# The second block's shift and scale rows: loaded and summed during attention by GpSimd, not during the first mixture by VectorE

## The chip, the cores and the metric

The kernel runs on one core of a Trainium2 chip, as one launch. The metric is the device time of an execution in microseconds (us). A core has a matrix engine (TensorE, PE), three engines for elementwise work (VectorE or DVE, ScalarE or ACT, GpSimd or POOL), SyncE (SP), which here issues the DMAs, and 16 DMA engines that move data between HBM and the on-chip memory (SBUF). TensorE writes to eight PSUM banks, `ps[0]` to `ps[7]`.

## The reference

Two transformer blocks follow each other on 256 tokens of width D = 1024, all in float32. Cut to what matters here:

```python
def first_block(x, c, ...):
    mod = silu(c) @ ada_w + ada_b                 # 1024 -> 6 x 1024: sh1 sc1 g1 sh2 sc2 g2
    h = rmsnorm(x, norm_mix) * (1 + sc1) + sh1
    x = x + g1 * diff_attention(h, ...)           # 8 heads
    h = rmsnorm(x, norm_ffn) * (1 + sc2) + sh2
    x = x + g2 * hier_moe(h, ...)                 # 16 experts, 2 for each token
    return rmsnorm(x, norm_final)

def second_block(x, c_2, ...):
    mod = silu(c_2) @ ada_w_2 + ada_b_2           # sh1, sc1: the first 2 x 1024 columns
    xn = rmsnorm(x, mix_norm_g_2) * (1 + sc1) + sh1
    ...                                           # projections, sparse attention, RWKV
    h = h + gt2 * hier_moe(...)                   # 32 experts
```

The change is about sh1 and sc1 of the second block: `silu(c_2)` (1024) times the first 2048 columns of `ada_w_2` (8 MiB).

## The kernel before, in words

P = 128 partitions, KC = D / P = 8. Each engine has its own instruction stream, and semaphores join them. The work runs in stages; the order within an engine is the order in which the functions of a stage are called: `start_*`, `attention_*`, `output_*`, `route_*` (the first routing), `pairs_*` (the first mixture of experts), then, behind a barrier of all engines (`give_back`), `project_*` and the rest of the second block.

A modulation vector is formed in two steps. The weight rows of one k (128 rows) are multiplied by `cond[:, k]`, one scalar per partition, and added up over k in SBUF, elementwise, on tiles of 128 partitions. Then TensorE sums over the partitions: `ada_columns` (L291) multiplies each block of 128 columns by a column of ones, eight matmuls with one moving column for each vector, and `fill_modc` (L573 to L575, VectorE) turns the result into the scale and shift in `modc`.

*The first block's vectors.* The pieces 0 to 7 of `ada_w` are summed on TensorE at the start. The pieces 8 to 23 (1 MiB each, two k of one vector) go through three slots of `side`; SyncE loads a piece (L194) when VectorE has used the one that lay in its slot, and VectorE sums them in attention with two instructions each (`ada_op`: L209 for the first k of a vector, else L215), 0 to 3 pieces a head by the list `ADA_STEPS = (0, 2, 2, 0, 3, 3, 3, 2, 1)`.

*Attention.* For each of 8 heads TensorE projects q, k and v, forms the scores of the head before it (L670), turns its probabilities (`turn`, L679) and multiplies by v (L689). VectorE adds the bias (L827), takes the maximum (L831), normalises (L841 to L844: `att_a`, for which `turn` waits) and takes the result (L850); ScalarE does the exponentials and copies. Between these VectorE's `fill` puts the modulation pieces. GpSimd has two iotas in attention and nothing else. SyncE's queue in attention: pieces 8 to 11, the cells 1, 3 and 5 of the projection weights, two bias rows, pieces 12 to 23, then half of `attn_w_out`, experts 0 and 2's cells and so on.

*First routing.* VectorE forms a mask of experts; TensorE turns it into positions (L1099 to L1103), VectorE makes one-hot tables from them, first that for gathering (`oh_first`), then `rounds`, then that for scattering (`oh_done`, which TensorE awaits at L1666).

*First mixture.* Experts go in eight pairs. TensorE gathers (L1609), projects by gate and up (L1620), down (L1628), scatters (L1646). The weights, 2 MiB for each matrix of an expert, lie in the ring of six cells and a spare cell of `side`; `load_rest` and `load_spared` (L1559) load the next pair's as this one's are used. Beside that, `ada2_side` runs once a pair: SyncE loads one k of the 2048 columns of `ada_w_2` (1 MiB, L1772) into `acc`, and VectorE adds it up (L1775), between the copy of the hidden values and the output of the down projection.

*Entry into the second block.* `project_tensor` begins with `ada_columns` for the two vectors (L291), `project_vector` waits for them behind the final norm of the first block and fills `modc`, and then norms again (L343 to L352) for TensorE's transposes.

`more` is a tile of 3840 columns that the RWKV recurrence of the second block uses, much later.

Of the kernel before, what the change touches and what calls it, by code (L numbers as in the profile page):

```python
# [19 lines left out]
P = 128  # L20
S = 256
D = 1024
# [25 lines left out]
def build(nc, inp, out, debug=None, until=99):  # L48
    ctx = ExitStack()
    with ctx:  # L50
# [65 lines left out]
        more = sb("more", 3840)  # L116
# [153 lines left out]
        def mod_columns2(pe, n, bank):  # L270
            vec = xn_sb[:, n * D:(n + 1) * D].rearrange("p (q c) -> p c q", c=KC)
            for c in range(KC):
                last = pe.matmul(bank[:, c:c + 1], vec[:, c, :], ones[:, 0:1], start=True, stop=True)
            last.then_inc(sem("modc2_psum"), 1)

# [332 lines left out]
        if True:  # L608
            def attention_sync(sp):
                load_ada(sp, range(8, 12))  # L610
                for i in (4, 5):
                    sp.wait_ge(sem(f"ada_used{i}"), 1)
                load_attn(sp, (1,))
                for i in (6, 7):
                    sp.wait_ge(sem(f"ada_used{i}"), 1)
                load_attn(sp, (3, 5))
                for i, m in enumerate((2, 5)):
                    sp.dma_start(g_b[:, i, :], inp["ada_b"][0:1, m * D:(m + 1) * D].broadcast_to((P, D))).then_inc(
                        sem("gb_loaded"), 16)
                load_ada(sp, range(12, 24))  # L620

                sp.wait_ge(sem("v_psum"), H // 2)
                sp.dma_start(cell(4), w_cols(inp["attn_w_out"][0], 0, 512)).then_inc(sem("wo1_loaded0"), 16)
                load_expert(sp, 0, (0, 2))
                sp.wait_ge(sem("v_psum"), H)
                sp.dma_start(cell(5), w_cols(inp["attn_w_out"][0], 512, 1024)).then_inc(sem("wo1_loaded1"), 16)
                load_expert(sp, 0, (1, 3))

            def attention_pool(pool):
                for t in range(NT):  # L630
                    last = pool.iota(dist[t], pattern=[[-1, S]], base=t * P, channel_multiplier=1,
                                     allow_small_or_imprecise_dtypes=True)
                    last.then_inc(sem("dist"), 1)

# [424 lines left out]
        def route(k, ne, has_bg):  # L1059
# [31 lines left out]
            if True:  # L1091
                def route_pool(pool):
                    pool.iota(prio, pattern=[[-1, 8]], base=8, channel_multiplier=0,
                              allow_small_or_imprecise_dtypes=True).then_inc(sem("prio"), 1)
                    pool.memset(acc[:, 0:2 * D], 0.0).then_inc(sem("ada2_cleared"), 1)

                def route_tensor(pe):
                    pe.wait_ge(sem("masked"), k + 1)
# [13 lines left out]
                def route_vector(v):  # L1112
# [66 lines left out]
                    v.tensor_scalar(rounds_i[:, :], rf[:, 0:1], 1.0, None, ALU.add).then_inc(sem(f"rounds{k}"), 1)  # L1179
                    pair_slots(v, tmp[:, 1280:1536], pos, gate).then_inc(sem(f"oh_done{k}"), 1)  # L1180
# [336 lines left out]
        def experts(k, ne, sides, afterwards):  # L1517
# [63 lines left out]
            def pairs_sync(sp):  # L1581
                sp.wait_ge(sem("rounds" + n), 1)
                sides(sp, 0)

                load_spared(sp, 1, 1, 1)
                with sp.Fori(1, NP // 2) as i:
                    for par in (1, 0):
                        it = 2 * i - par
                        load_spared(sp, it + 1, it + 1, 1 - par)
                        load_rest(sp, it, it, par)  # L1590
                        sides(sp, it)
                load_rest(sp, NP - 1, NP - 1, 1)
                sides(sp, NP - 1)
# [125 lines left out]
            def pairs_vector(v):  # L1719
# [11 lines left out]
                def body(it, side):  # L1731
# [11 lines left out]
                    if side is not None:  # L1743
                        side(v, it)
# [8 lines left out]
                v.wait_ge(sem("ada2_cleared"), 1)  # L1753
                with v.Fori(0, NP) as it:
                    body(it, sides)
                with v.If(rounds > 1):
                    with v.Fori(NP, rounds * NP) as it:
                        body(it, None)
                v.nop()
# [5 lines left out]

        def ada2_side(eng, it):

            ws, a = acc[:, 2 * D:4 * D], acc[:, 0:2 * D]
            if eng is nc.sync:
                if not isinstance(it, int) or it:  # L1770
                    eng.wait_ge(sem("ada2_row_used"), it)
                eng.dma_start(ws, inp["ada_w_2"][0][bass.ds(it * P, P), 0:2 * D]).then_inc(sem("ada2_row_loaded"), 16)  # L1772
            else:
                eng.wait_ge(sem("ada2_row_loaded"), 16 * it + 16)
                eng.scalar_tensor_tensor(a, ws, cond[:, bass.ds(it + KC, 1)], a, ALU.mult, ALU.add).then_inc(  # L1775
                    sem("ada2_row_used"), 1)
# [10 lines left out]
        pairs_sync, pairs_tensor, pairs_scalar, pairs_vector = experts(0, 16, ada2_side, after_first)  # L1787
# [178 lines left out]
        if True:  # L1966
# [55 lines left out]
            def project_tensor(pe):  # L2022
                ada_columns(pe, (0, 1), ps[0], "modc_psum")
# [76 lines left out]
            def project_vector(v):  # L2100
# [3 lines left out]
                v.wait_ge(sem("modc_psum"), FIRST_COLS + 3)  # L2104
                fill_modc(v, 3, 0, KC, ps[0][:, 0:KC], ps[0][:, KC:2 * KC], colA("mix_norm_g_2", 0, KC), colB("ada_b_2", 0, KC), colB("ada_b_2", KC, KC))
# [1164 lines left out]
```

## Time and profile before

| | us |
|---|---|
| median of 3 runs | 1293.92 |
| lowest, highest | 1291.79, 1298.25 |
| the profiled execution | 1294.76 |
| its span | 1292.6 |
| TensorE busy | 1035.1 (80%) |
| VectorE busy | 463.6 (36%) |
| ScalarE busy | 235.9 (18%) |
| GpSimd busy | 43.0 (3%) |

The span is what the profile records of the execution; 2.2 us lie around it. Busy time is that of instructions that do work; waits are not in it. The stages that the text speaks of lie at these times of the span: attention to about 162, output projection to 195, routing to 212, first mixture to 470, entry into the second block from 470 on. PEclk is the granted clock of TensorE, 1.00 for 2.4 GHz.

### The profile page before, as it was taken

The page shows a single profiled execution, that of the slowest core. Times are in us where ns is not written, and L with a number is a line of the kernel's source. Part 1 is how long each engine was busy: PE and PEld are TensorE (multiplying, and loading weights), DVE is VectorE, ACT ScalarE, POOL GpSimd, SP SyncE. Part 2 cuts the span into 40 slices and gives each one's busy share as a digit, 9 for nine tenths or more (in the row PEclk, how much of TensorE's full clock was granted, in tenths as well). Part 3 has the DMA queues.
Part 4 walks back from the last instruction along what each step waited for, and adds up shares of the span by engine and source line. Part 5 has one row for each costly group of instructions (what it writes and reads, how often), then busy time and mean ns, then how long its engine had stood idle before and what let it go on. Part 6 is the DMA issues. An engine that isn't in the chain of part 4 may idle for free.

```text
span 1292.6 us, 15349 instructions
## 1 busy us (share of the span) xinstructions
PE 1035.1 (80%) x6075; PEld 605.6 (47%) x6075; DVE 463.6 (36%) x1142; ACT 235.9 (18%) x575; POOL 43.0 (3%) x91
## 2 busy tenths in 40 slices
PE   4899997999999979989999999694654647474647
PEld 1788844444333456856788685451212113131213
DVE  1369824232222246876853463521010101010211
ACT  2133312111111131224521200120101010010101
POOL 0000000000000020000010500000000000000000
PEclk9899897999999979989999999898878778786878
DMA  9785935999999969711314108789999999999997
GB/s 370 246 335 196 396 112 213 371 429 427 427 427 428 429 236 388 292 66 66 131 38 139 67 23 308 298 329 425 423 424 423 422 427 419 429 421 428 421 428 292
DMA packets 76892, 406.10 MB, mean 314 GB/s; under 512 B 18633, under 2 KB 19974, under 8 KB 54184
## 3 DMA queue, kind: packets, MB, share of 16 engines
q1 hardware_dynamic: 76840, 405.38, 77.5%
q8 instruction: 36, 0.59, 0.2%
q14 instruction: 16, 0.13, 0.0%
HBM read 403.14 MB, written 2.23 MB: 314 GB/s over the span
## 4 chain that ended last, share of the span: by engine, by line
PE 30%; DMA 25%; DVE 6%; issue 1%; ACT 0%; SPq 0%; POOL 0%; DVEq 0%
DMA ring<-in_expert_w_up 11%; DMA ring<-in_expert_w_gate 7%; DMA ring<-in_expert_w_down 7%; PE ps L1247 5%; PE ps L2663 3%; PE ps L1884 3%; PE ps L3139 2%; PE ps L1287 2%; PE ps L2911 1%; PE ps L3129 1%; PE ps L1263 1%; PE ps L2032 1%; PE ps L1228 1%; PE ps L2742 1%; PE ps L2675 1%
## 5 line engine op out<-in xcount | busy, mean ns | idle before, releaser
L1247 PE MATMUL ps<-ring,hT_sb 128*32 128x512 f32 x672 | 127.8, 743 | 163.1 <-DMA side<-in_expert_w_gate 53.6
L1247 PEld LDWEIGHTS ps<-ring,hT_sb 128*32 128x32 f32 x672 | 32.8, 133 | 252.5 <-issue 252.5
L1620 PE MATMUL ps<-ring,hT_sb 128*64 128x512 f32 x448 | 113.2, 595 | 3.4 <-DMA ring<-in_expert_w_gate 3.4
L1374 DVE TENSOR_TENSOR tmp<-ps,tmp 128x512 f32<-128x512 f32 x8 | 5.5, 692 | 194.7 <-ACT tmp L1362 194.7
L644 PE MATMUL ps<-hT_sb,ring 128*128 128x256 f32 x256 | 62.3, 393 | 4.1 <-DMA ring<-in_attn_w_in 4.1
L1247 PE MATMUL ps<-side,hT_sb 128*32 128x512 f32 x224 | 61.3, 710 | 0.0
L1620 PEld LDWEIGHTS ps<-ring,hT_sb 128*64 128x64 f32 x448 | 35.4, 137 | 55.0 <-issue 54.9
L1353 ACT ACTIVATE hT_sb<-ps,modc 128x128 f32<-128x128 f32 x72 | 27.1, 457 | 181.4 <-PE ps L1228 181.4
L1884 PE MATMUL ps<-hT_sb,ring 128*128 128x256 f32 (+1 forms) x240 | 59.8, 405 | 0.0
L1628 PE MATMUL ps<-ring,tmp 128*64 128x512 f32 x256 | 56.7, 595 | 0.0
L644 PEld LDWEIGHTS ps<-hT_sb,ring 128*128 128x128 f32 x256 | 48.0, 194 | 15.3 <-issue 4.6
L1884 PEld LDWEIGHTS ps<-hT_sb,ring 128*128 128x128 f32 (+1 forms) x240 | 45.9, 197 | 10.5 <-issue 3.6
L1702 ACT ACTIVATE hT_sb<-ps,modc 128x128 f32<-128x128 f32 x72 | 27.1, 457 | 122.5 <-PE ps L1609 122.5
L1287 PE MATMUL ps<-ring,tmp 128*32 128x512 f32 x360 | 43.5, 595 | 3.3 <-DMA ring<-in_expert_w_down 3.3
L1362 ACT ACTIVATE tmp<-ps 128x512 f32<-128x512 f32 x8 | 4.8, 597 | 222.6 <-PE ps L1247 218.4
L2663 PE MATMUL ps<-hT_sb,ring 128*128 128x256 f32 x192 | 42.5, 380 | 0.0
L1228 PE MATMUL ps<-tmp,xn_sb 128*128 128x128 f32 x288 | 36.6, 289 | 2.7 <-DVE tmp L1045 2.7
L2663 PEld LDWEIGHTS ps<-hT_sb,ring 128*128 128x128 f32 x192 | 36.1, 190 | 5.4 <-issue 0.7
L1609 PE MATMUL ps<-tmp,xn_sb 128*128 128x128 f32 x288 | 36.4, 288 | 1.7 <-DVE tmp L1055 1.7
L1228 PEld LDWEIGHTS ps<-tmp,xn_sb 128*128 128x128 f32 x288 | 35.8, 206 | 2.9 <-DVE tmp L1045 2.9
L1609 PEld LDWEIGHTS ps<-tmp,xn_sb 128*128 128x128 f32 x288 | 35.6, 205 | 1.8 <-DVE tmp L1055 1.8
L1381 DVE TENSOR_TENSOR tmp<-ps,tmp 128x512 f32<-128x512 f32 x8 | 5.5, 692 | 85.9 <-PE ps L1247 82.6
(510 smaller groups left out, 1628.5 us busy)
## 6 DMA issues: line engine op xcount, KB each, us to landing
ring<-in_expert_w_down SPq DMA_DIRECT2D x24, 2048.0 KB, 16.5
ring<-in_expert_w_gate SPq DMA_DIRECT2D x12, 4096.0 KB, 20.7
ring<-in_expert_w_up SPq DMA_DIRECT2D x12, 4096.0 KB, 31.7
ring<-in_expert_w_up SPq DMA_DIRECT2D x16, 2048.0 KB, 18.5
ring<-in_expert_w_down SPq DMA_DIRECT2D x7, 4096.0 KB, 19.9
ring<-in_expert_w_gate SPq DMA_DIRECT2D x12, 2048.0 KB, 19.6
side<-in_ada_w SPq DMA_DIRECT2D x20, 1024.0 KB, 6.3
ring<-in_w_in SPq DMA_DIRECT2D x9, 2048.0 KB, 8.0
```

Source lines behind the costliest of these rows:

```text
L644: last = pe.matmul(ps[6][:, w * S:(w + 1) * S], cell(2 * w + h // 4)[:, c, (h % 4) * P:(h % 4 + 1) * P], hT[:, c, :], start=(c == 0), stop ...
L1228: last = pe.matmul((gate_ps, up_ps)[half][:, (c % 4) * P:(c % 4 + 1) * P], xn3[:, t, c * P:(c + 1) * P], oh[:, t, :], start=(t == 0), stop ...
L1247: last = pe.matmul(bank[es, :], xg[:, c, es], w[e][:, c, :], start=(c == 0), stop=(c == KC - 1))
L1287: last = pe.matmul(out_ps[h][es, :], hidT[:, f, es], right, start=(f == 0), stop=(f == FC - 1))
L1353: last = act.activation(xg[:, c, :], (gate_ps, up_ps)[half][:, (c % 4) * P:(c % 4 + 1) * P], ACT.Identity, scale=modc[:, 2 * KC + c:2 * KC ...
L1609: last = pe.matmul((gate_ps, up_ps)[half][:, (c % 4) * P:(c % 4 + 1) * P], xn3[:, t, c * P:(c + 1) * P], oh[:, t, :], start=(t == 0), stop ...
L1620: last = pe.matmul(bank[e * SLOTS:(e + 1) * SLOTS, :], xg[:, c, e * SLOTS:(e + 1) * SLOTS], dst(e, j, par)[:, c, :], start=(c == 0), stop= ...
L1628: last = pe.matmul(out_ps[h][e * SLOTS:(e + 1) * SLOTS, :], hidT[:, f, e * SLOTS:(e + 1) * SLOTS], dst(e, 2, 0)[:, f, h * 512:(h + 1) * 51 ...
L1702: last = act.activation(xg[:, c, :], (gate_ps, up_ps)[half][:, (c % 4) * P:(c % 4 + 1) * P], ACT.Identity, scale=modc[:, 2 * KC + c:2 * KC ...
L1884: last = pe.matmul(ps[SHIFT_BANKS[m]][0:n, 0:S], p2(i)[:, c, o:o + n], hT[:, c, :], start=(c == 0), stop=(c == KC - 1))
L2663: last = pe.matmul(gate_bank(i)[:, 0:S], p2(GATE0 + m // 4)[:, c, (m % 4) * P:(m % 4 + 1) * P], hT[:, c, :], start=(c == 0), stop=(c == KC ...
L3139: last = pe.matmul(ps[g][:, :], mrg[:, c, t * P:(t + 1) * P], out_w[n][:, c, :], start=(c == 0), stop=(c == KC - 1))
```

## The change

The rows of `ada_w_2` for shift and scale are loaded in attention, in sixteen loads of 0.5 MiB (one k, one vector), into the upper half of `more`, one place for each vector. GpSimd multiplies each by its scalar and adds it to the sum in the lower half of `more` (`sum_rows2`, behind the two iotas). A load waits until the row that lay in its place has been used. In SyncE's queue two of them stand behind piece 11, two behind the cells 3 and 5, and then one behind each of the pieces 12 to 23. The sixteen column sums (`row_columns2`) stand at the head of `route_tensor` and write `ps[7]`; `fill_modc` for them stands behind `rounds` in `route_vector`. The loads and sums in the mixture go, with the memset on GpSimd that cleared their sum, and VectorE's loop over the pairs is one in place of two. `more` grows to 4096 columns, and the scratch for dynamic DMAs shrinks from 1024 to 256.

```diff
@@ -113,7 +113,7 @@
-        more = sb("more", 3840)
+        more = sb("more", 4096)
@@ -272,6 +272,41 @@
+        row_sums = more[:, 0:2 * D]
+        def row_piece(i):
+            return more[:, (2 + i) * D:(3 + i) * D]
+        def load_rows2(sp, k, i):
+            if k:
+                sp.wait_ge(sem(f"row_used{i}"), k)
+            sp.dma_start(row_piece(i), inp["ada_w_2"][0][k * P:(k + 1) * P, i * D:(i + 1) * D]).then_inc(sem(f"row_loaded{i}"), 16)
+        def sum_rows2(pool):
+            for k in range(KC):
+                for i in range(2):
+                    a, s = row_sums[:, i * D:(i + 1) * D], cond[:, KC + k:KC + k + 1]
+                    pool.wait_ge(sem(f"row_loaded{i}"), 16 * k + 16)
+                    if k == 0:
+                        pool.wait_ge(sem("cond"), 1)
+                        ins = pool.tensor_scalar(a, row_piece(i), s, None, ALU.mult)
+                    else:
+                        p_step(pool.tensor_scalar(row_piece(i), row_piece(i), s, None, ALU.mult))
+                        pool.wait_ge(sem(f"row_used{i}"), k)
+                        ins = pool.tensor_tensor(a, a, row_piece(i), ALU.add)
+                    ins.then_inc(sem(f"row_used{i}"), 1)
+        def row_columns2(pe, bank):
+            for i in range(2):
+                pe.wait_ge(sem(f"row_used{i}"), KC)
+                for c in range(KC):
+                    last = pe.matmul(bank[:, i * KC + c:i * KC + c + 1], row_sums[:, i * D + c * P:i * D + (c + 1) * P],
+                                     ones[:, 0:1], start=True, stop=True)
+            last.then_inc(sem("modc_psum"), 1)
@@ -608,17 +643,22 @@ attention_sync
                 load_ada(sp, range(8, 12))
+                load_rows2(sp, 0, 0)
+                load_rows2(sp, 0, 1)
...
                 load_attn(sp, (3, 5))
+                load_rows2(sp, 1, 0)
+                load_rows2(sp, 1, 1)
...
-                load_ada(sp, range(12, 24))
+                for i in range(12):
+                    load_ada(sp, (12 + i,))
+                    load_rows2(sp, 2 + i // 2, i % 2)
@@ -631,6 +671,7 @@ attention_pool
+                sum_rows2(pool)
@@ -1092,9 +1133,9 @@ route
-                    pool.memset(acc[:, 0:2 * D], 0.0).then_inc(sem("ada2_cleared"), 1)
                 def route_tensor(pe):
+                    row_columns2(pe, ps[7])
                     pe.wait_ge(sem("masked"), k + 1)
@@ -1177,6 +1218,9 @@ route_vector
                     v.tensor_scalar(rounds_i[:, :], rf[:, 0:1], 1.0, None, ALU.add).then_inc(sem(f"rounds{k}"), 1)
+                    v.wait_ge(sem("modc_psum"), FIRST_COLS + 3)
+                    fill_modc(v, 3, 0, KC, ps[7][:, 0:KC], ps[7][:, KC:2 * KC], colA("mix_norm_g_2", 0, KC), colB("ada_b_2", 0, KC),
+                              colB("ada_b_2", KC, KC))
                     pair_slots(v, tmp[:, 1280:1536], pos, gate).then_inc(sem(f"oh_done{k}"), 1)
@@ -1580,17 +1624,13 @@ pairs_sync
-                sides(sp, 0)
...
-                        sides(sp, it)
...
-                sides(sp, NP - 1)
@@ -1740,8 +1780,6 @@ body, on VectorE
-                    if side is not None:
-                        side(v, it)
@@ -1750,30 +1788,13 @@
-                v.wait_ge(sem("ada2_cleared"), 1)
-                with v.Fori(0, NP) as it:
-                    body(it, sides)
-                with v.If(rounds > 1):
-                    with v.Fori(NP, rounds * NP) as it:
-                        body(it, None)
-                v.nop()
+                with v.Fori(0, rounds * NP) as it:
+                    body(it)
...
-        def ada2_side(eng, it):
-            ws, a = acc[:, 2 * D:4 * D], acc[:, 0:2 * D]
-            if eng is nc.sync:
-                if not isinstance(it, int) or it:
-                    eng.wait_ge(sem("ada2_row_used"), it)
-                eng.dma_start(ws, inp["ada_w_2"][0][bass.ds(it * P, P), 0:2 * D]).then_inc(sem("ada2_row_loaded"), 16)
-            else:
-                eng.wait_ge(sem("ada2_row_loaded"), 16 * it + 16)
-                eng.scalar_tensor_tensor(a, ws, cond[:, bass.ds(it + KC, 1)], a, ALU.mult, ALU.add).then_inc(
-                    sem("ada2_row_used"), 1)
@@ -2020,7 +2041,6 @@ project_tensor
-                ada_columns(pe, (0, 1), ps[0], "modc_psum")
@@ -2101,8 +2121,6 @@ project_vector
-                v.wait_ge(sem("modc_psum"), FIRST_COLS + 3)
-                fill_modc(v, 3, 0, KC, ps[0][:, 0:KC], ps[0][:, KC:2 * KC], ...)
@@ -3255,7 +3273,7 @@
-    nc = bacc.Bacc("TRN2", ..., dynamic_dma_scratch_size=1024)
+    nc = bacc.Bacc("TRN2", ..., dynamic_dma_scratch_size=256)
```

## Rows read from the trace of the kernel before

**Rows 1.** Windows: us, PE, PEld, DVE, ACT, POOL busy (x count), PEclk, DMA, GB/s.
```profile
278.00:308.00 30.00, 29.14 (x144) 12.53 (x142) 7.96 (x16) 4.90 (x10) 0.00 (x0) 1.00 1.01 427
```
**Rows 2.** Timeline of SyncE's queue in the mixture: start, us, line, transfer.
```profile
278.02 0.81 SPq L1559 DMA_DIRECT2D ring<-in_expert_w_down  x2
...
307.95 0.81 SPq L1559 DMA_DIRECT2D ring<-in_expert_w_down  x2
...
369.72 0.81 SPq L1559 DMA_DIRECT2D ring<-in_expert_w_down  x2
...
401.55 0.81 SPq L1559 DMA_DIRECT2D ring<-in_expert_w_down  x2
```
**Rows 3.** Waits in the mixture: who waited for whom, us in total, times, longest.
```profile
PE ps L1620 <- DMA ring<-in_expert_w_gate: 5.1, 3, 1.7
```
**Rows 4.** Timelines of VectorE and TensorE in attention: start, us, instruction.
```profile
111.91 0.48 DVE L844 SCALAR_TENSOR_TENSOR acc<-acc,gate_t 128x256 f32<-128x256 f32 x1
...
112.83 0.38 PE L679 MATMUL ps<-ident,acc 128*128 128x128 f32 x2
...
126.30 0.38 PE L679 MATMUL ps<-ident,acc 128*128 128x128 f32 x2
```
**Rows 5.** Windows of two heads, without and with three pieces.
```profile
80.20:93.60 13.40, 13.40 (x86) 11.30 (x85) 5.88 (x19) 4.55 (x16) 0.00 (x0) 1.00 0.92 363
93.60:107.00 13.40, 13.40 (x85) 11.33 (x84) 12.50 (x25) 4.52 (x16) 0.00 (x0) 1.00 0.36 123
```
**Rows 6.** SyncE's waits from 60 to 136 us, and its queue behind them.
```profile
SPq L194 <- DVE acc L215: 67.0, 10, 21.8
...
133.60 0.47 SPq L623 DMA_DIRECT2D ring<-in_attn_w_out  x1
```
**Rows 7.** GpSimd's groups by shape: count, busy us, mean ns, idle before.
```profile
L2647 POOL TENSOR_TENSOR side<-side,gate_t 128x256 f32<-128x256 f32 x32 | 19.0, 625 | 162.1 <-ACT side L2506 97.3 <-PE ps L2742 64.8
L3159 POOL TENSOR_TENSOR gate_rows<-gate_rows,side 1x2048 f32<-1x2048 f32 x1 | 4.5, 4502 | 3.4 <-DMA side<-in_ada_b 3.4
...
L2418 POOL MEMSET acc<- 128x1024 f32 x1 | 1.0, 952 | 0.0
```
**Rows 8.** Timelines of VectorE and GpSimd; the line L2860: min, median, max ns.
```profile
473.02 1.28 DVE L354 SCALAR_TENSOR_TENSOR x_sb<-x_sb,small,gate_rows 128x1024 f32<-128x1024 f32 x1
473.23 1.25 POOL L2003 TENSOR_SCALAR_AFFINE_SELECT pos_t<-pos_t 128x128 f32<-128x128 f32 x1
...
714.79 0.67 DVE L2860 TENSOR_TENSOR ring<-more,gate_t 128x256 f32<-128x256 f32 x1
...
714.56 0.62 POOL L2647 TENSOR_TENSOR side<-side,gate_t 128x256 f32<-128x256 f32 x1
...
L2860 DVE TENSOR_TENSOR ring<-more,gate_t x16: 411/424/833, 703.6 to 730.0; 128x256 f32<-128x256 f32 x16
```
**Rows 9.** Timeline of the routing and of the entry into the second block.
```profile
207.50 0.61 PE L1099 MATMUL ps<-mask_t,before 128*128 128x16 f32 x2 [4.84 <-DVE mask_t L1155]
...
470.53 6.96 PE L291 MATMUL ps<-ones,acc 128*128 128x1 f32 x32 [3.59 <-PEq L73]
...
476.16 1.06 ACT L326 ACTIVATE xn_sb<-x_sb 128x1024 f32<-128x1024 f32 x1 [0.51 <-DVE x_sb L354]
...
478.75 0.78 DVE L352 TENSOR_SCALAR xn_sb<-x_sb,small 128x1024 f32<-128x1024 f32 x1
```
**Rows 10.** VectorE's groups from 93.6 to 147 us: count, busy us, mean ns.
```profile
L215 DVE SCALAR_TENSOR_TENSOR acc<-side,cond,acc 128x1024 f32<-128x1024 f32 x19 | 24.3, 1280 | 0.5
...
L844 DVE SCALAR_TENSOR_TENSOR acc<-acc,gate_t 128x256 f32<-128x256 f32 x8 | 3.9, 485 | 0.3
...
L843 DVE TENSOR_SCALAR acc<-acc,gate_t 128x256 f32<-128x256 f32 x8 | 2.7, 343 | 0.0
...
L209 DVE TENSOR_SCALAR acc<-side,cond 128x1024 f32<-128x1024 f32 x3 | 2.2, 747 | 0.0
```
**Rows 11.** Window behind a gap on TensorE.
```profile
194.00:198.00 4.00, 2.63 (x15) 2.03 (x17) 3.11 (x6) 1.42 (x4) 0.00 (x0) 0.50 1.02 434
```

More of the change, by code:

```diff
@@ L1515, in route_quads, with experts @@
             return route_pool, route_tensor, route_scalar, route_vector
-        def experts(k, ne, sides, afterwards):
+        def experts(k, ne, afterwards):
             NP = ne // 2
@@ L1729, in slots_of, with body @@
                     last.then_inc(sem("oh_done" + n), 1)
-                def body(it, side):
+                def body(it):
                     v.wait_ge(sem("sig_done" + n), it + 1)
@@ L1786, in build @@
         route_pool, route_tensor, route_scalar, route_vector = route(0, 16, True)
-        pairs_sync, pairs_tensor, pairs_scalar, pairs_vector = experts(0, 16, ada2_side, after_first)
+        pairs_sync, pairs_tensor, pairs_scalar, pairs_vector = experts(0, 16, after_first)
         with nc.Block() as block:
@@ L2103, in project_vector @@
                     rms_vector(v, 2, t, x3, weight=g_b[:, 0, :], name="x_ready")
-                v.wait_ge(sem("modc_psum"), FIRST_COLS + 3)
-                fill_modc(v, 3, 0, KC, ps[0][:, 0:KC], ps[0][:, KC:2 * KC], colA("mix_norm_g_2", 0, KC), colB("ada_b_2", 0, KC), colB("ada_b_2", KC, KC))
                 for t in range(NT):
@@ L3256 @@
     from concourse.bass_utils import run_bass_kernel_spmd
-    nc = bacc.Bacc("TRN2", target_bir_lowering=False, num_devices=1, dynamic_dma_scratch_size=1024)
+    nc = bacc.Bacc("TRN2", target_bir_lowering=False, num_devices=1, dynamic_dma_scratch_size=256)
     arrays, inp = {}, {}
```

## The prediction, made before the changed kernel ran

> **What bounds the kernel now.** I read three things in this order: the kernel in stretches, then who waited for whom, then single instructions. The change touches three stretches.
>
> *First mixture (236 to 470 us), where work is taken away.* The DMA engines are full there, 1.01 busy at 427 to 429 GB/s, and each period of two experts moves 12 MiB of weights plus 1 MiB of `ada_w_2` rows, 13.6 MB [rows 1]. But TensorE is busy 29.1 to 29.3 us of each period too. The SyncE issues show which of the two ends last. The first periods are 29.93 us long (278.02 to 307.95, and again to 337.89), the next ones 31.83 us (to 369.72, then to 401.55) [rows 2]. At 428 GB/s 13.6 MB take 31.8 us. So TensorE's own pace is 29.93, transfers lag behind it, the loads made ahead cover that for some periods, and then three projections wait for a gate transfer, 5.1 us in total [rows 3].
>
> *Attention (53 to 147 us), where work is put in.* A head takes 13.47 us: the turn L679 comes at 112.83, 126.30, and so on [rows 4]. TensorE is busy throughout. VectorE is busy 5.9 us of a head without modulation pieces and 12.3 to 12.5 us of one with three pieces [rows 5]. Its slack in such a head is less than the idle 1 us. The turn at 112.83 needs the product L844 that started at 111.91 and takes 0.48, so 0.4 us is free on that path [rows 4]. GpSimd is idle. The DMA engines have holes (0.36 busy from 93.6 to 107, and 0.34, 0.92, 0.63 and 0.62 in the other four heads from 53.4 to 133.8) [rows 5], because SyncE's loads wait 67.0 us in total for VectorE to free a slot [rows 6].
>
> *Routing and the entry into the second block.* Before the masks L1155 come, TensorE is idle 4.84 us; 16 column sums (x32 instructions) take 6.96 us at 470.53 [rows 9].
>
> **The change part by part.**
>
> *1. Eight 1 MiB loads leave the mixture.* The period then carries 12.6 MB, 29.4 us at 428 GB/s, under TensorE's 29.93. The three periods that lasted 31.83 to 31.87 go back to 29.93: 3 x 1.9 = **-5.7 us**. The bulk of the 19.6 us of transfer that go (8.39 MB at 428 GB/s) is worth nothing, since TensorE is next. The eight VectorE sums of 2.35 us (L1775) lie inside the down projection, where VectorE waits 4.2 us for L1628 anyway: 0. Bounds of this part: 5.1 us (the waits alone) to 5.8.
>
> *2. Sixteen loads of 0.5 MiB enter attention.* At 390 GB/s they are 21.5 us of transfer, against holes that sum to 28 us in those five heads. The two ahead of cells 1, 3, 5 delay these by 2.7 us; issued from 61.5 on, their 6 MiB need 16 us, and they are used from the fifth head on, after 91: 0. In the queue a row waits for GpSimd to have used the row before it, and behind it stand the next `ada_w` piece and in the end `attn_w_out`. In a stretch without contention GpSimd needs 3.4 us for a row (below) and VectorE 4.5 us for a piece, so the row is not the slower one: 0, and if it is, that is a part of rival three. The first half of `attn_w_out` is issued at 133.60 [rows 6] and used from 162 on: with its 5.4 us of transfer some 20 us to spare.
>
> *3. GpSimd's sums.* 16 multiplications of 128x1024 and 14 additions of 128x1024. No such operation is in the trace. The addition: 128x256 takes 0.61 us and 2048 columns 4.50, so 2.17 ns a column, 1024 columns 2.28 us. The multiplication reads one tensor: a memset of 1024 columns takes 0.95 (lower end), the addition 2.28 (upper end); I take 1.1, near the memset [rows 7]. Sum 16 x 1.1 + 14 x 2.28 = 49.5 us. Alone this is off every path. The question is what it does to VectorE.
>
> The trace shows it at two places [rows 8]. An affine_select on GpSimd, 0.31 us on the same tile a moment before, started at 473.23 and took 1.25 us: to 474.48, just behind the end (474.30) of a VectorE product with two SBUF inputs of 128x1024 (L354, from 473.02). And the other way round: VectorE's L2860 (two SBUF inputs, median 0.424) started at 714.79 while a GpSimd addition ran from 714.56 to 715.18, and ended at 715.46, 0.67 us, 0.28 behind the addition. So one waits for the other until it ends. The longest of these VectorE products is 0.83 us (its median stands in the row of the line).
>
> Now price it in heads four to seven, 93.6 to 147 us (53.4 us). VectorE's instructions that take two SBUF inputs, or are tensor_scalar from SBUF to SBUF, sum to 24.3 + 3.9 + 2.7 + 2.2 = 33.1 us there [rows 10]. The rows of k = 2 to 7 fall into the same stretch, one behind each piece: 12 x (1.1 + 2.28) = 40.6 us. Together 73.7 us in a stretch of 53.4: **+20 us** if all that VectorE does without that conflict (16 us) is hidden below GpSimd's instructions. With no overlap at all it is 49.5 + 40.6 - 53.4 = +37; with the last two rows falling behind the stretch and the full overlap +13; if the two places above don't carry over to longer instructions, 0. A wait of even 2 us within a head reaches TensorE, since the turn has 0.4 us [rows 4], and TensorE has nothing to make it up with (busy all of the stretch). I take +20. It isn't given back later: the output projection starts on the last head, the routing on that, and SyncE's first mixture loads on the routing.
>
> The Trainium skill, page "SBUF — State Buffer", section "Who interferes with whom", speaks against the change: GpSimd shares a port pair with VectorE's second one, held as an exclusive lock for the whole instruction, against VectorE instructions with two SBUF inputs or in a two-port mode. The two places of rows 8 agree. By that rule this part is the +20 above; by a rule of shared bandwidth it would be a few us.
>
> *4. The columns move into the routing.* 16 column sums behind L311, which ends at 202.65: 202.65 + 6.96 = 209.6. The position matmuls L1099, now at 207.50, wait for that: **+2.1 us**, and with them the positions and the first gather. VectorE's waiting there (0.4 us before L1172) doesn't cover it. The three small VectorE sums of the fill, 0.5 us, stand behind `rounds` and ahead of `oh_done`, which is needed at 228.4: 0. The memset of 1.8 us on GpSimd was in nobody's way: 0. Bounds: 0 (were the matmuls to run in the idle time at full clock) to 2.5.
>
> *5. The entry into the second block.* The fill at 477.53 waited for L291. Without it, the next thing late is ScalarE's second square (476.16 to 477.31), behind which its root stands; that root moves from 478.31 to 477.3, and the first product from 478.75 to 477.75: **-1.0 us** [rows 9]. The granted clock was 0.50 all through these sums, so they had warmed nothing; were the clock to rise at the same time as before and not with the transposes, the gain is up to 1 us smaller.
>
> *6.* One loop in place of two, the smaller scratch: no instruction on a path, 0.
>
> Sum: -5.7 + 20 + 2.1 - 1.0 = +15.4. The profiled execution took 1294.76 us (span 1292.6 and 2.2 around it), 0.84 above the median 1293.92 of three runs (1291.79 to 1298.25); so about **1310 us**.
>
> **Rivals.**
>
> *Two: no contention worth the name.* GpSimd's sums run beside VectorE, as instructions of 0.6 us did with little harm over heads of 13.47 us. For it: rows 8 show it on few instructions, all short on one side. Against it: both directions show a wait up to the other's end. Then -5.7 + 2.1 - 1.0 + 0 to 3 = -4.6 to -1.6: **1290 to 1293**, not slower. It decides if VectorE's long products keep 1.28 us. Half of the contention (GpSimd yields and its tail runs into the last head and the projection) gives 1300.
>
> *Three: contention, and TensorE's clock or the loads fall with it.* Behind a gap of 4.5 us on TensorE, which ended at 195.37, the granted clock was 0.50, 1.2 GHz [rows 11]. If a head's waits add up to one such gap, part of each of five heads runs at 1.2 instead of 2.4 GHz; 4 us of such work cost 2 more, 10 in all. The same price has a SyncE queue in which a row that isn't used yet holds up the next piece (2 us for each of five heads). **1320**. For it: the extra per head is 5 us. Against: it comes in pieces of 1 to 2.3 us.
>
> *Four: the mixture gives more than I see.* If the gate waits of rows 3 understate the lag and the entry and the routing cost nothing, and GpSimd is harmless, -5.8 - 1.0 = -6.8, or 1288. Nothing in the profile gives more, since TensorE's 29.93 us stand.
>
> **Chances.** The forecast 0.58, two 0.22 (a third of it the halfway case at 1300), three 0.15, four 0.05. About 0.5% (6.5 us) is what a measurement of this kernel can tell from no change: below 1287.5 is faster, above 1300.4 slower. Slower: 0.58 + 0.15 + a little of two, less the part of the forecast that ends low: 0.73. Faster 0.05, within 0.22. The likeliest case has its own range 1303 to 1322; the range for 8 in 10 reaches down into rival two and up over rival three: 1290 to 1326.
>
> **What would show it.** The period between SyncE's down loads stays at 29.93 us to the end and the gate waits of rows 3 are gone (1). GpSimd's additions take 2.3 us or more, and L215's mean rises from 1.28 to 1.8 us or more; the head's period goes from 13.47 to some 18 us from the fifth head on, and L679 waits for VectorE (3). L1099 starts 2 us behind its mask (4). L352 starts 1 us sooner behind the barrier (5). I am wrong if L215 stays at 1.28 us, or if it rises and the heads still take 13.5 us.

## The result, and the profile after

The changed kernel takes **1320.34 us** (median of 4, 1319.08 to 1322.88) against 1296.09 for the kernel before (4 runs, 1291.79 to 1298.96, two of them above 1298): ratio 1.0204, 95% interval 1.0182 to 1.0226. It is 2% slower, 10 us above the 1310 that was forecast and within the range of 1290 to 1326. In the later comparisons the kernel before had medians of 1292.9 to 1293.9 with 7 to 23 runs, so its four runs here stand a little high; against those the loss is 26.5 to 27.5 us. The profiled executions are 1322.88 and 1294.76, 28.1 apart.

Where the two profiles part, by the start of the same work (after less before):

```
output projection, first matmul      189.7 - 162.3 = +27.4 us
position matmuls of the routing      235.0 - 207.5 = +27.5
barrier behind the first mixture     492.4 - 470.5 = +21.9
first projection of block two        505.4 - 484.5 = +20.9
end of its DMA-bound stretch (L2214) 590.3 - 567.0 = +23.3
transposes of L2451                  673.2 - 644.4 = +28.8
end of the span                                      +28.5
```

The groups of VectorE from 53 to 175 us, with busy us, mean ns and idle before (before: the first stands in [rows 10] at 1280 ns, the second at 485, the third at 343):

```profile
L215 DVE SCALAR_TENSOR_TENSOR acc<-side,cond,acc 128x1024 f32<-128x1024 f32 x26 | 44.6, 1717 | 0.7
L885 DVE SCALAR_TENSOR_TENSOR acc<-acc,gate_t 128x256 f32<-128x256 f32 x14 | 15.0, 1068 | 0.5
L884 DVE TENSOR_SCALAR acc<-acc,gate_t 128x256 f32<-128x256 f32 x14 | 9.7, 692 | 0.0
L874 DVE TENSOR_SCALAR gate_t<-gate_t 128x2 f32<-128x2 f32 x15 | 6.3, 423 | 0.5
```

Over the whole program, all 28 instructions of L215 grew from 1280 to 1686 ns, the 16 of L885 from 484 to 995, of L884 from 344 to 649, of L874 from 169 to 407, the 4 of L209 from 747 to 947: 11.4 + 8.2 + 4.9 + 3.8 + 0.8 = 29.1 us. That is enough for the 27.4 us by which the output projection is late. Idle time before L215 is no longer than before, so VectorE never waited for a piece: it was slower.

The windows of two heads' worth of time (PE, PEld, DVE, ACT, POOL busy, clock, DMA), to be read beside [rows 5]: GpSimd is busy 13.23 of 13.4 us, VectorE 13.12 where it had slack, and TensorE, full before, has holes.

```profile
93.60:107.00 13.40, 11.38 (x72) 9.28 (x70) 12.46 (x19) 4.02 (x15) 13.23 (x5) 1.00 0.77 271
107.00:120.40 13.40, 9.49 (x47) 6.92 (x45) 13.12 (x18) 2.12 (x8) 13.23 (x5) 1.00 0.77 253
```

The waits from 60 to 180 us name who it was (total, times, longest):

```profile
PE ps L720 <- DVE acc L885: 15.0, 6, 6.0
```

The timelines of GpSimd, VectorE and TensorE (start, us) show the collision in the single instruction. Here L884 and L885 run beside a GpSimd multiplication (98.95 to 101.80) and then an addition (101.88 to 104.23):

```profile
98.95 2.85 POOL L297 TENSOR_SCALAR more<-more,cond 128x1024 f32<-128x1024 f32 x1
99.23 0.98 DVE L884 TENSOR_SCALAR acc<-acc,gate_t 128x256 f32<-128x256 f32 x1
100.25 0.48 DVE L885 SCALAR_TENSOR_TENSOR acc<-acc,gate_t 128x256 f32<-128x256 f32 x1
100.97 0.97 DVE L884 TENSOR_SCALAR acc<-acc,gate_t 128x256 f32<-128x256 f32 x1
101.88 2.35 POOL L299 TENSOR_TENSOR more<-more 128x1024 f32<-128x1024 f32 x1
101.98 2.53 DVE L885 SCALAR_TENSOR_TENSOR acc<-acc,gate_t 128x256 f32<-128x256 f32 x1
...
116.84 1.29 DVE L215 SCALAR_TENSOR_TENSOR acc<-side,cond,acc 128x1024 f32<-128x1024 f32 x1
116.88 3.88 POOL L297 TENSOR_SCALAR more<-more,cond 128x1024 f32<-128x1024 f32 x1
...
123.52 0.69 PE L720 MATMUL ps<-ident,acc 128*128 128x128 f32 x2 [5.97 <-DVE acc L885]
...
147.73 3.81 POOL L297 TENSOR_SCALAR more<-more,cond 128x1024 f32<-128x1024 f32 x1
148.96 1.93 DVE L215 SCALAR_TENSOR_TENSOR acc<-side,cond,acc 128x1024 f32<-128x1024 f32 x1
...
158.17 2.35 POOL L299 TENSOR_TENSOR more<-more 128x1024 f32<-128x1024 f32 x1
159.58 0.96 DVE L874 TENSOR_SCALAR gate_t<-gate_t 128x2 f32<-128x2 f32 x1
```

*Under an addition.* Of the rows of L885 that show a single instruction, all four that start within an addition take 2.52 to 2.54 us, ending 0.28 behind it. L215 takes 3.16 to 3.28 when it starts with 2 us of the addition to run (four of four). The small L874 waits as well: all four that start within an addition take 0.77 to 0.96 instead of 0.17 and end 0.02 behind it.

*Under a multiplication.* All four L885 that start 1.3 to 1.5 us into one keep 0.48, and so do the L215 that start 1.8 us or more into one (1.28). But the five L215 that start in its first 1.3 us take 1.93 to 2.14, and end before it does. L884 takes 0.88 to 0.98 there (eight of eight; 0.34 alone).

*The other way round.* A multiplication that starts while an L215 runs takes 3.81 to 3.92 us instead of 2.85 (six of six). Without one it takes 2.84 to 3.02, whether products start within it or not. Additions that start under a product are lengthened too, from 2.35 to at most 2.93. So the harm depends on the pair and on the order: GpSimd's two-input addition holds VectorE off to its end, products and L874 alike; its one-input multiplication holds a product only when this starts early in it, and adds about 0.6 us to L884.

SyncE's down loads in the mixture, now the same distance apart to the end (before: [rows 2]), 29.94 and 29.94 us:

```profile
275.69 0.81 SPq L1603 DMA_DIRECT2D ring<-in_expert_w_down  x2
305.63 0.82 SPq L1603 DMA_DIRECT2D ring<-in_expert_w_down  x2
...
425.37 0.81 SPq L1603 DMA_DIRECT2D ring<-in_expert_w_down  x2
455.31 0.81 SPq L1603 DMA_DIRECT2D ring<-in_expert_w_down  x2
```

The routing and the entry (before: [rows 9]): the column sums take 3.63 us at full clock and end 1.4 us before the masks, so they cost nothing.

```profile
230.03 3.63 PE L307 MATMUL ps<-ones,more 128*128 128x1 f32 x32
235.04 0.61 PE L1140 MATMUL ps<-mask_t,before 128*128 128x16 f32 x2 [1.38 <-DVE mask_t L1196]
...
500.46 3.68 PE L398 MATMUL ps<-ident,xn_sb 128*128 128x128 f32 x16 [11.63 <-DVE xn_sb L387]
```

### The profile page after: what moved, and what is told of

The parts are those of the page before. It is cut to its first block, busy times and chain, and to the rows that moved or that the text cites. A ratio compares the mean times of both kernels' runs of the same rounds, so it can differ in the third digit from the quotient of the medians.

```text
span 1321.1 us, 15364 instructions
## 1 busy us (share of the span) xinstructions
PE 1045.7 (79%) x6075; PEld 611.1 (46%) x6075; DVE 472.7 (36%) x1134; ACT 236.1 (18%) x575; POOL 130.1 (10%) x120
## 4 chain that ended last, share of the span: by engine, by line
DMA 28%; PE 25%; DVE 6%; issue 2%; ACT 1%; SPq 0%; POOL 0%; DVEq 0%
DMA side<-in_expert_w_down 9%; DMA side<-in_expert_w_up 8%; DMA side<-in_expert_w_gate 7%; PE ps L1291 5%; PE ps L2681 3%; DMA side<-in_ada_w 3%; PE ps L1905 2%; PE ps L3157 2%; PE ps L2929 1%; DMA ring<-in_expert_w_gate 1%; PE ps L3147 1%; DVE xn_sb L242 1%; PE ps L1307 1%; PE ps L2760 1%; PE ps L2693 1%
## 5 line engine op out<-in xcount | busy, mean ns | idle before, releaser
L1418 DVE TENSOR_TENSOR tmp<-ps,tmp 128x512 f32<-128x512 f32 x8 | 5.5, 692 | 192.4 <-ACT tmp L1406 192.4
L297 POOL TENSOR_SCALAR more<-more,cond 128x1024 f32<-128x1024 f32 x14 | 46.6, 3326 | 14.4 <-DMA more<-in_ada_w 14.4
L215 DVE SCALAR_TENSOR_TENSOR acc<-side,cond,acc 128x1024 f32<-128x1024 f32 x28 | 47.2, 1686 | 0.8
L698 PE MATMUL ps<-ring,hT_sb 128*128 128x128 f32 x256 | 37.2, 309 | 3.3 <-DMA ring<-in_attn_w_in 3.3
## 6 DMA issues: line engine op xcount, KB each, us to landing
ring<-in_expert_w_up SPq DMA_DIRECT2D x16, 2048.0 KB, 12.1
```

Source lines behind the costliest of these rows:

```text
L215: ins = v.scalar_tensor_tensor(a, w, s, a, ALU.mult, ALU.add)
L297: p_step(pool.tensor_scalar(row_piece(i), row_piece(i), s, None, ALU.mult))
L698: last = pe.matmul(ps[7][:, t * P:(t + 1) * P], hT[:, c, t * P:(t + 1) * P], cell(4 + h // 4)[:, c, (h % 4) * P:(h % 4 + 1) * P], start=(c ...
```

## The experiments

Theory one: GpSimd and VectorE hold each other up at SBUF. Its rival, **the queue**: SyncE waits for GpSimd before each row, and the `ada_w` pieces behind come late. Milestones below are of the profiled execution, less the kernel before; a minus is earlier.

**E1, signals alone.** Loads and waits stay; the sums go.

```
-  p_step(pool.tensor_scalar(row_piece(i), row_piece(i), s, None, ALU.mult))
-  ins = pool.tensor_tensor(a, a, row_piece(i), ALU.add)
+  ins = pool.memset(row_piece(i)[:, 0:1], 0.0)
```

> The changed kernel, but behind each row from k = 1 on GpSimd clears one column and signals; the multiplications and additions of k = 1 to 7 are left out (14 of 16 rows are not in the sums). Loads, queue, columns and fill stay. Theory one (port: GpSimd's sums and VectorE's instructions wait for each other) and theory two (queue: GpSimd's slow sums hold up the ada_w pieces behind them in SyncE's queue) both say that attention goes back to 13.47 us a head and L215 to 1.28 us. It prices the rest of the change: 1294.8 - 5.7 (mixture) - 1.0 (entry) + 0 (columns, hidden at full clock) = 1288. If the 16 loads in attention had a price of their own, it would be above 1292.

Measured 1292.29 us against 1293.82 (0.9988, 0.9976 to 1.0000). Output projection +1.2, L215 back at 1280 ns:

```profile
L215 DVE SCALAR_TENSOR_TENSOR acc<-side,cond,acc 128x1024 f32<-128x1024 f32 x28 | 35.8, 1280 | 0.8
```

The two multiplications of k = 0 are still in E1, and under them VectorE's products and tensor_scalar of 256 columns grew by 1.4 us in all, about the delay. So the sixteen loads have no price of their own that shows here; what GpSimd does with the rows costs the rest. E1 also shows the mixture's gain lost again: first projection of block two -3.9, end -0.6.

**E2, writes only.** GpSimd as busy as with the sums, by memsets of the row tile (no sums).

```
-  p_step(pool.tensor_scalar(...))         +  3 x p_step(pool.memset(row_piece(i), 0.0))
-  ins = pool.tensor_tensor(...)           +  2 x the same, and one of 384 columns
```

> The changed kernel, with GpSimd's multiplication of 2.85 us replaced by three clears of 128x1024 (0.95 us each) and its addition of 2.35 us by two and a part, so that GpSimd is busy as long but reads nothing (the sums of k = 1 to 7 are left out). Theory one: VectorE's products with two SBUF inputs keep 1.28 us, since nothing reads beside them; only its tensor_scalar instructions might still wait; total 1290 to 1300. Theory two: GpSimd is as slow for SyncE's queue as before, the pieces come each 5 to 6 us, total 1312 to 1320.

Measured 1305.04 (1.0089, 1.0071 to 1.0106), between the two ranges; output projection +11.3. The groups of VectorE:

```profile
L215 DVE SCALAR_TENSOR_TENSOR acc<-side,cond,acc 128x1024 f32<-128x1024 f32 x28 | 35.8, 1280 | 3.3 <-DMA side<-in_ada_w 2.6
L887 DVE TENSOR_SCALAR acc<-acc,gate_t 128x256 f32<-128x256 f32 x16 | 9.7, 609 | 0.0
L885 DVE RECIPROCAL gate_t<-gate_t 128x2 f32<-128x2 f32 x16 | 4.3, 270 | 0.2
```

Two-input products aren't touched by a GpSimd that only writes; tensor_scalar (344 ns before) and even a reciprocal of two columns (162) are. Of the 12.1 us by which its profile ends late, 5.0 came in a stretch of block two at 1.2 GHz (see E4).

**E3, the same sums in instructions of 256 columns.**

```
+  for j in range(4): ... pool.tensor_scalar(r, r, s, None, ALU.mult)   # 256 columns each
+  for j in range(4): ... pool.tensor_tensor(a[:, c4], a[:, c4], row_piece(i)[:, c4], ALU.add)
```

> The changed kernel, each GpSimd instruction of 1024 columns cut into four of 256; same result, same columns read and written. Theory one in its form of occupancy (GpSimd's whole reading time and VectorE's add up): GpSimd's total grows by the fixed part of 48 more instructions of each kind, so no gain, 1320 to 1335. In its other form (what costs is the tail of a long instruction in front of a short VectorE one on the critical path) the wait in front of each falls to a fourth: 1300 to 1312.

Measured 1337.86 (1.0358, 1.0338 to 1.0378): worse, and above both ranges. VectorE's products are hurt less (1485 ns against 1686), but a row now takes GpSimd four times 1.1 + 0.9 = 8.0 us in the mean, and here the queue shows, as VectorE's wait for its own pieces:

```profile
L215 DVE SCALAR_TENSOR_TENSOR acc<-side,cond,acc 128x1024 f32<-128x1024 f32 x28 | 41.6, 1485 | 24.8 <-DMA side<-in_ada_w 24.5
```

**E6, contention without the queue.** No row loads, no waits of SyncE; GpSimd sums zeros from the sixth unit of attention on.

```
-  every load_rows2(sp, ...) and pool.wait_ge(sem(f"row_loaded{i}"), ...)
+  pool.wait_ge(sem("att_biased"), 6)      # once, ahead of the sums
```

> The sums' 30 GpSimd operations run back to back from the sixth attention unit on, on data already in memory: the 16 row loads and every wait of SyncE for GpSimd are left out (so the sums are of zeros). Theory one, contention (GpSimd and VectorE slow each other at SBUF): nearly the whole loss in attention stays, output projection 20 to 27 us later than before, the 28 VectorE sums of L215 at 1600 to 1700 ns, time 1312 to 1318. Rival, the queue (SyncE waits for GpSimd before each load, and the ada pieces behind it come late): with no such wait the output projection starts as before, the 28 sums keep 1280 ns, time 1290 to 1293.

Measured 1319.14 (1.0201, 1.018 to 1.0223; two runs at 1316.2, two at 1322.1 and 1322.9), output projection +26.1, 1715 ns for L215: nearly the whole loss in attention without any queue.

```profile
L215 DVE SCALAR_TENSOR_TENSOR acc<-side,cond,acc 128x1024 f32<-128x1024 f32 x28 | 48.0, 1715 | 0.8
L882 DVE SCALAR_TENSOR_TENSOR acc<-acc,gate_t 128x256 f32<-128x256 f32 x16 | 16.7, 1041 | 0.6
```

**E7, the queue without contention.** All loads and waits, GpSimd's time filled by one-column memsets (rows 4.4 to 7.2 us apart, the sums' own 5.3 to 6.9; GpSimd holds a row 4.4 us where the sums held it 5.2, so it is a somewhat milder queue).

```
-  p_step(pool.tensor_scalar(...))    +  16 x p_step(pool.memset(row_piece(i)[:, 0:1], 0.0))
-  ins = pool.tensor_tensor(...)      +  13 x the same
```

> The changed kernel with its 16 row loads and all its waits, each GpSimd multiplication replaced by 16 chained memsets of one column and each addition by 13 (about 0.18 us each by the spacing of the after profile, so about 2.9 and 2.3 us): GpSimd holds SyncE's queue as long as the sums did but hardly touches SBUF (the sums are left out). Theory one, contention: time as with signals alone, 1291 to 1294, 28 VectorE sums at 1280 ns. Rival, the queue: output projection 20 us or more late, idle time of VectorE on the ada pieces above 10 us, time 1312 to 1320.

Measured 1300.11 (1.0047, 1.0032 to 1.0061), output projection +9.4: neither number. The queue alone is worth some 8 us over E1:

```profile
L215 DVE SCALAR_TENSOR_TENSOR acc<-side,cond,acc 128x1024 f32<-128x1024 f32 x28 | 35.8, 1280 | 7.4 <-DMA side<-in_ada_w 6.7
```

But it isn't added to the contention: E6 without a queue is 1.2 us from the changed kernel in the output projection, since a VectorE that needs longer for each piece has the next piece in time.

**E4, the mixture alone.** The kernel before without the side loads and sums, nothing in their place.

```
-  experts(0, 16, ada2_side, after_first)
+  experts(0, 16, lambda eng, it: None, after_first)
```

> The kernel before with the mixture's eight 1 MiB loads and its eight VectorE sums left out and nothing put in their place (the second block's shift and scale are then the bias alone). Prediction part 1 alone: period 31.83 to 29.93 us in three of the seven periods, barrier 5.7 us earlier, time 1288 to 1289. Rival, the second block gives it back (its own ada_w_2 loads start relative to the barrier and its queue is no shorter): barrier 5.7 us earlier but the end only 2 to 4 us earlier, time 1290 to 1292.

Measured 1293.33 (0.9987, 0.9977 to 0.9998), above both ranges; its ten times are 1288.15, 1290.12 and eight from 1292.99 to 1294.27. Its profile is 8.3 us early at the first projection of block two (1.6 of them from ahead of the mixture), 5.4 at L2214, and 0.1 at L2451. Even with all the work gone, the change could hardly have gained as the kernel stands. The last 5 us went here, in what is called the cold stretch below: 10 us in which the granted clock is 0.50, that is 1.2 GHz. TensorE's timeline and windows (PE busy, clock, DMA share, GB/s):

```profile
612.45 0.63 PE L2246 MATMUL ps<-side,acc 128*128 128x64 f32 x4 [0.67 <-DVE side L2369]
613.66 1.09 PE L2272 MATMUL ps<-ident,side 128*128 128x128 f32 x8 [0.57 <-DVE side L2369]
...
614.90:616.90 2.00, 2.00 (x8) 0.52 1.04 402
616.90:618.90 2.00, 2.00 (x10) 0.50 0.62 221
```

The kernel before has the same two waits (0.67 and 0.58 us) at the same place, and goes on at 2.4 GHz:

```profile
620.00:622.00 2.00, 2.00 (x14) 1.00 1.05 407
```

The profiles of the changed kernel (clock 0.50 from 645 us on) and of E2 have the cold stretch too, those of E1, E3, E6 and E7 don't.

**E11 and E12, those waits filled.** Four idle matmuls of 128x256, in E4 and in the changed kernel.

```
+  def keep_busy(pe):
+      for n in range(2):
+          pe.matmul(ps[4][:, n * S:(n + 1) * S], ident[:, :], hT[:, n, :], start=True, stop=True)
+  keep_busy(pe)       # ahead of av(15), and ahead of pe.wait_ge(sem("sa_o"), 16)
```

> The kernel without the mixture's loads and sums, plus four matmuls of 128x256 (two ahead of the last value product, two ahead of the transposes of the second attention's output, L2246 and L2272 of the kernel before), where TensorE sat idle 0.67 and 0.58 us before a clock of 1.2 GHz set in for about 10 us in its profile. Theory: that cold stretch (5 us, present in most executions without the filler and absent in the rest) is what takes the mixture's gain back; with the waits filled it is gone from every execution: 1288 to 1290, no spread into two groups. Rival: the clock falls all the same (it depends on what came before, at 605 us), 1293 with some executions at 1288, as without the filler.

E11: 1289.53 against 1292.86 (0.9975, 0.9964 to 0.9985), eight runs from 1288.35 to 1291.48 and no second group. The place in its profile:

```profile
615.00:617.00 2.00, 2.00 (x14) 1.00 1.05 410
```

> The changed kernel with only the four filler matmuls in the second block. Its profile held the cold stretch (4.4 us between the matmuls of L2426 and L2451 of the kernel before). Theory: the stretch is in most executions of it, so the filler takes 3 to 5 us off: 1315 to 1317, and what is left, 22 to 24 us over the kernel before, is the contention less the mixture's gain. Rival: it was in the profiled execution alone, and the time stays at 1319 to 1321.

E12: 1317.44 (1314.96 to 1319.61; 1.0181, 1.0164 to 1.0198), 2.9 us under the changed kernel's 1320.34, but that is from another comparison and the intervals of the two ratios overlap. Its profile goes from +24.3 at L2214 to +24.7 at L2451, where the changed kernel's went from +23.3 to +28.8. So the stretch is gone from the profile, and its share of the median stays between 0 and 5 us; 24.6 us over the kernel before are left.

**E5, E9, E10: VectorE makes the sums in its own waits.** In the kernel before, VectorE waits 6.0, 5.4, 2.5 and 6.3 us in the output projection for the four halves of y, which my prediction never looked at. Eight loads of 1 MiB at the end of attention, sums of 2.35 us there, the columns in the routing as in the change.

```
-  sum_rows2(pool)
   for g in (2 * t, 2 * t + 1):
+      for k in ((0, 1), (2, 3), (4,), (5, 6, 7))[g]:
+          sum_rows2(v, k)          # scalar_tensor_tensor over 2048 columns
       residual(v, g, 0, "y1")
```

> A version without GpSimd: rows in eight loads of 1 MiB, k = 0 and 1 behind piece 14 (DMA hole), 2 and 3 behind attn_w_out, 4 to 7 behind the router's loads (hole from 172 to 190); VectorE sums them (2.35 us each) where it waits for the output projection, 20.1 us of waits before. Columns and fill as in the changed kernel. Theory one: no conflict, attention keeps 13.47 us a head, total 1294.8 - 5.7 - 1.0 = 1288, up to 1292 if the last sums delay the norm by a few us. Theory two: the same.

E5: 1297.17 (1.0027, 1.0018 to 1.0036), above its range: nothing gained but the contention gone. Two things cost. The last residual comes behind the sums before it: 191.93 us against 190.92 in the kernel before, though the output projection started 1.6 us earlier, so it is 2.6 us late. And its profile has the cold stretch (+5).

```profile
187.21 4.81 DVE L301 SCALAR_TENSOR_TENSOR acc<-side,cond,acc 128x2048 f32<-128x2048 f32 x2
191.93 0.68 DVE L947 TENSOR_TENSOR tmp<-ps,gate_rows 128x512 f32<-128x512 f32 x1
```

E9 splits the sums 3, 2, 1, 2 and loads the fifth piece ahead of the router's rows:

```
+  for k in ((0, 1, 2), (3, 4), (5,), (6, 7))[g]:
+  load_rows2(sp, 4)                # into acc[:, 3 * D:5 * D], ahead of load_router
```

> VectorE makes the eight sums in its waits of the output projection, now 3, 2, 1 and 2 of them ahead of the four residuals (before: 2, 2, 1, 3), with the fifth piece loaded ahead of the router's rows into free space, so no sum waits for its DMA more than 0.3 us and the last residual is not late. Theory: routing starts as in the kernel before (positions within 0.5 us, 1.7 late in the version with 2, 2, 1, 3), barrier 5 to 6 us early, and the end 2 to 4 us early if no cold stretch of TensorE appears in the second block (1290 to 1292), 1295 to 1297 if one does. Rival: the sums on VectorE cost what the mixture's loads gave, 1294 to 1298 whatever the split.

E9: 1297.94 (1.0021, 1.0007 to 1.0035), in two groups again (four at 1292.25 to 1295.20, eight at 1297.34 to 1299.79). My reasoning on the load was wrong: issued at 155.76 with the router's rows behind it, it was waited for until 179.65, and the routing started 4.7 us late. SyncE was busy for 19.22 us with issuing one of the router's loads (L941), right behind it.

```profile
155.76 0.43 SPq L299 DMA_DIRECT2D acc<-in_ada_w  x1
...
179.65 2.35 DVE L309 SCALAR_TENSOR_TENSOR acc<-acc,cond 128x2048 f32<-128x2048 f32 x1 [5.96 <-DMA acc<-in_ada_w]
```

E10 is E5 with the eighth sum in the wait for the router's logits, and E11's filler:

```
+  for k in ((0, 1), (2, 3), (4,), (5, 6))[g]:
+  sum_rows2(v, 7)                  # in route_vector, ahead of the wait for "prio"
+  keep_busy(pe)                    # as in E11
```

> The version with VectorE's sums, with the eighth sum moved out of the last residual's wait into the wait for the router's logits (2.67 us idle there, the sum 2.35), and the same filler in the second block. Theory: residual not late, routing starts within 0.5 us of the kernel before, barrier 5 to 6 us earlier, second block gives back 2 to 3 us in its DMA-bound stretch and nothing to the clock: 1289 to 1292, below both kernels. Rival: the filler doesn't hold the clock, 1294 to 1296.

E10: **1290.19 us** (1288.26 to 1291.37) against 1292.86: 0.9975, 0.9965 to 0.9986, with nothing left out. It is 0.25% faster than the kernel before, and as fast as E11, which leaves the work out. The kernel before with the filler alone wasn't run. But E10's profile is already 4.5 us early at L2214, ahead of the filler, so the filler isn't what gains there. The last residual is on time and the eighth sum hides:

```profile
190.64 0.69 DVE L947 TENSOR_TENSOR tmp<-ps,gate_rows 128x512 f32<-128x512 f32 x1
...
198.25 2.35 DVE L301 SCALAR_TENSOR_TENSOR acc<-side,cond,acc 128x2048 f32<-128x2048 f32 x1
```

**E8, the scratch.** The kernel before with `more` at 4096 columns and the scratch at 256.

> The kernel before with only the tile widened to 4096 columns and the dynamic DMA scratch cut to 256. Prediction part 6: no effect, 1293 to 1295, second block unchanged. Rival: the smaller scratch is what makes the loads after the barrier slower (w_kv_up's issue 2 us instead of 0.6, the first matmuls after the DMA-bound stretch 1.5 to 2 us later relative to the barrier), 1295 to 1297.

Measured 1294.09 against 1292.86 (1.001, 1.0001 to 1.0019), 1.2 us where 0 stood (interval 0.1 to 2.5). Its profile nevertheless ends 1.0 us early. Its barrier comes 2.4 us early, with two gate waits instead of three in a mixture that is unchanged, and block two gives 2.2 of that back by L2214.

## Why the prediction was right, and what in it was not

*Part 1, the mixture.* Right: period 29.94 us to the end, no wait for a gate transfer, barrier 27.5 - 21.9 = 5.6 us nearer (forecast 5.7). One profile of an unchanged mixture (E8) has two gate waits where the kernel before has three, so up to 1.6 us of this may be variation between executions.

*Part 2, the loads.* Right: E1's output projection is 1.2 us late, and the 1.4 us that GpSimd's two multiplications cost VectorE there account for it.

*Part 3, the sums.* The mechanism was right, and E6 and E1 show it: sums without a queue bring the loss, and the loads and waits without the sums don't. The size wasn't. The multiplication takes 2.85 us unobstructed, not 1.1, and lies outside the bounds 0.95 to 2.28: two rows of other operations don't bound a third one. The addition was right (2.35 against 2.28). The formula then erred the other way: with 2.85 it would have given 12 x (2.85 + 2.28) + 33.1 - 53.4 = +41, because it took every pair of the two lists to exclude each other. Only the addition does so to the end; a multiplication delays a product that starts in its first 1.3 us by 0.65 to 0.86 us, and a later one not at all. The rule that I drew on from the Trainium skill, page "SBUF — State Buffer", section "Who interferes with whom" (a lock held for the whole instruction), agrees with the four products under additions and not with the four under multiplications, which kept 0.48 us; the measurement decides. Two errors of opposite sign left +20 beside a measured +27.4; that it came so near is luck.

*Part 4, the columns.* Wrong: 0 instead of +2.1. The step "16 column sums take 6.96 us" took the duration from a row at 1.2 GHz and put it into a place where TensorE has just worked; at 2.4 GHz they took 3.63 and fit the idle 4.84 us of [rows 9]. The bound of 0 named this.

*Part 5, the entry.* -1.0 measured, as forecast. E4 keeps the columns and is 1.0 early too: they took 5.61 us there instead of 6.96, and the fill no longer waited for them. So the gain comes as soon as these sums are a little shorter; they needn't leave.

*What the sum left out.* It stopped at the entry and took every gain ahead of it as kept. Block two gave back 2.4 us in its DMA-bound stretch (2.8 in E4, 2.7 in E11, 3.1 in E1, 3.2 in E7), and 5 us in the cold stretch where it came. So the -5.7 and the -1.0 together were worth 3.3 us with the filler (E11) and 0.5 without (E4), with GpSimd left out altogether. In the profiled pair the parts are +27.4 (forecast +20), 0 (+2.1), -5.6 (-5.7), -1.0 (-1.0), and +2.4 and +5.5 that the sum didn't have: 28.7, against 28.5 at the end of the span.

*The rivals.* Two and four fell with E6. Three has the measured time, but not for its reasons: in attention VectorE's own growth (29.1 us) accounts for the delay, all that the changed kernel has over E6 there is 1.2 us, and the clock was 1.00 in the two windows shown; its share came in the second block, at a place that the rival didn't name.

*Open.* Why the stretch up to L2214 gives back 2.3 to 3.2 us in all versions without the side loads: there VectorE waits longer for its `ada_w_2` pieces (12.37 us in E4, 10.12 before), and SyncE issues the third piece 16.6 to 17.6 us behind the barrier instead of 16.0. The scratch isn't needed for it, since E4 and E11 have the old one. The missing side loads aren't either: E8 has them, and it issues the third piece at 17.1 and gives back 2.2 us. What all of these share is a mixture that ends sooner behind the routing than in the one profile of the kernel before; how much of it is variation between executions isn't known. What decides in one execution whether the clock falls behind the same two waits wasn't found either; only that with both filled, the two groups of times were gone (E11).

## What to carry to other kernels

Here an idle engine wasn't free, since its instructions held up those of a full one. Before work is moved to GpSimd, list VectorE's instructions in that stretch by kind, and ask of each pair which of the two waits and for how long; a short trial with that pair tells more than rows of other operations. Look first for waits of the engine that already does the work; here VectorE had 20 us of them. A gain ahead of a DMA-bound or clock-sensitive stretch counts only as far as that stretch passes it on, so follow it to the end of the program.

## What the hardware showed that I had not expected

- Which of the two waits, and how long, depends on the GpSimd operation: under an addition of two tensors a VectorE product waited to 0.28 us behind its end (2.53 instead of 0.48 us), under a multiplication by a scalar it kept 0.48 when it started 1.3 us or more into it (changed kernel).
- A GpSimd tensor_scalar over 128x1024 f32 with a scalar per partition takes 2.85 us, longer than an addition of two tensors (2.35); a memset of the same size takes 0.96 (E2).
- GpSimd instructions that only write slow VectorE's tensor_scalar (344 to 609 ns) and reciprocal (162 to 270), and leave a two-input product of 1024 columns at 1280 ns (E2).
- Shorter GpSimd instructions reduce the harm per VectorE instruction but cost 0.92 us (multiplication) and 0.73 us (addition) for 256 columns in the median, 29% and 24% more than a quarter of the unobstructed long ones; with VectorE in the way the means are 1.11 and 0.90 (E3).
- Two waits of 0.6 us on TensorE can cost 5 us of the program's time, by the times in most executions of some versions (eight of ten in E4) and in none of the eight where they were filled (E11).
